# Three sets of seven-product column groups in each feed-forward unit of a one-core two-stack transformer

## The chip, the cores and the metric

One core of a Trainium2 chip runs one program. The metric is the device time of that program in microseconds; inputs lie in the chip's memory (HBM) and every weight is read once. TensorE multiplies, ScalarE and VectorE round, copy, gate and add, GpSimd does small work, SyncE's queue loads the weights.

## What is computed

The reference runs two small stacks one after the other over 256 rows of width 1024, in float32: mixers (attention, state-space scan, gated recurrence, MLA, GQA) and behind each of the four of them a feed-forward unit, the part that the change is about. The first stack's unit is, cut to its core:

```python
def swiglu(x, w_gate, w_up, w_down):
    return (jax.nn.silu(x @ w_gate) * (x @ w_up)) @ w_down
x = x + rms_norm(swiglu(rms_norm(x, norm_ffn_pre), w_gate, w_up, w_down), norm_ffn_post)
```

with a hidden width of 2816. The second stack's units have the same three products. All products are wanted to nearly float32.

## The kernel before, in words

**Products.** A float32 product is made of three in fp32r: each operand is rounded to a high part, and the rest is kept as a low part; `mm3` (L520) issues high x high, high x low and low x high (L521 to L523), each with 128 rows, 128 of the contraction and 512 columns. Below, "a product" is these three matmuls.

**Weights.** All weight matrices are packed into chunks of 128 x 2048 numbers in the order of use. SyncE loads chunk c into RAW[c % 3] (`weights`, L3072). ScalarE rounds it into WH[c % 3] (`split_hi`, L1364), VectorE subtracts to get the rest in WL[c % 3] (`split_lo`, L2050). On both engines `feed(c)` (L1366, L2052) makes all splits up to chunk c + 3 that aren't made yet, each as soon as TensorE has counted the chunk three before it as done (`S.used`). Where a `feed` stands among an engine's other work is written out by hand, and each engine works strictly in that order. TensorE waits for the rest of a chunk with `rests_ready` (L492).

**A feed-forward unit** (`ffn`, L832 on TensorE, L1467 on ScalarE, L2223 on VectorE) goes over 11 groups of 256 hidden columns, gate and up side by side, 512 columns of a PSUM bank for each half t of the rows. A plain group is two chunks of 8 products. ScalarE then applies Silu (`tanh`, L1471), VectorE multiplies (`gate`, L2227) into AN, and TensorE transposes AN in a `fold` (L836; four transposes) that ScalarE and VectorE copy out as high and low part (L1491, L2250). For g in FAST = (2, 4, 6, 8) a fold also makes sums of quarters: ScalarE keeps one quarter (`kept`, L1487), VectorE does five small operations (`form_sums`, L2236), ScalarE copies twice. Then the down projection (`wide_mm`) takes 11 chunks.

**Sets.** SETS = (2, 6): groups a and a + 1 are computed together from four chunks cs[2a] to cs[2a+3]. Each of two of these chunks ("fast" chunks, those in FASTS) is done with 7 products instead of 8, by sums of blocks of the activations (`forms`, L2264, once a unit) and of the weights (`sums`, L2117: four VectorE operations of 512 columns in YG; rounded by ScalarE in `sums_hi`, L1432; their rests in `sums_lo`, L2132). A fast chunk's split leaves out its first 512 columns. `set_mm` (L756) goes plain, fold, fast, plain, fast. The seven products go to separate banks, and VectorE puts them together with eight operations of 512 columns (`combine_first`, `combine_second`, L2156 and L2170).

**Order by hand.** On each engine `column_set(a)` (L1516, L2294) holds the set's work, and the end of `ffn` calls it between groups and folds. The fold ahead of the set stands at its head, in front of `feed(cs[2a])`:

```python
                def column_set(a):
                    fold(a - 1)
                    feed(cs[2 * a])
                    sums_hi(cs[2 * a + 3])
                    feed(cs[2 * a + 1])
```

`decay_rates` (L2614), 28 operations on 128 x 8 numbers, is put behind groups 8, 9 and 10 of ffn 0; ScalarE needs the result in the gated recurrence (L1854), some 100 us later.

Of the kernel before, what the change touches and what calls it, by code (L numbers as in the profile page):

```python
# [267 lines left out]
def program(nc, A, PLAN, NCH):  # L268
# [10 lines left out]
    with top:  # L279
# [239 lines left out]
        def pe(e):  # L519
# [188 lines left out]
            def early_chunk(f, a, first, c):  # L708

                m, i = FASTS[c], 0 if first else 1  # L710
                GSh, GSl = FB[f][8:10]
                k = 2 if first else 6
                W = lambda n: (WH[:, c % NW, 512 * n:512 * n + 512], WL[:, c % NW, 512 * n:512 * n + 512])
                T = lambda n: (TGh[:, n, :], TGl[:, n, :])
                Y = lambda j, t: (HTh[:, k + j, 128 * t:128 * t + 128], HTl[:, k + j, 128 * t:128 * t + 128])
                S_ = lambda n: (GSh[:, i, 128 * n:128 * n + 128], GSl[:, i, 128 * n:128 * n + 128])

                def mul(b, x, w, own):
                    return mm3(PS[:, b, :], *x, *w, own and first, not first)

                def side(b, x, w):
                    tk = mul(b, x, w, False)
                    if not first:
                        tk.then_inc(S.ms, 1)

                def top_left():
                    return mul(5, Y(0, 0), W(1), True)

                def with_sum(b, n):
                    e.wait_ge(S.tlo, 4 * m + T_ORDER.index(n) + 1)  # L730
                    return mul(b, *((S_(0), S_(1), S_(2), Y(1, 1))[n], T(n)), n < 3)

                rests_ready(e, c)
                e.wait_ge(S.gsl, 2 * f + i + 1)
                if first:
                    side(0, Y(1, 0), W(2))
                    side(1, S_(3), W(3))
                    e.wait_ge(S.an, gt_n(f, a - 1, 1))
                    with_sum(6, 1).then_inc(S.tu, 1)
                    with_sum(7, 2).then_inc(S.tu, 1)  # L740
                    with_sum(2, 3)
                    e.wait_ge(S.ylo, fold_n(f, a - 2))
                    with_sum(4, 0).then_inc(S.tu, 1)
                    e.wait_ge(S.ylo, fold_n(f, a - 1))
                    tk = top_left()
                else:
                    top_left().then_inc(S.ms, 1)
                    with_sum(6, 1).then_inc(S.tu, 1)
                    with_sum(4, 0).then_inc(S.tu, 1)
                    side(0, Y(1, 0), W(2))  # L750
# [2405 lines left out]
```

## Time and profile before

| | |
|---|---|
| median of 3 runs | 1228.4 us (1227.89 to 1228.4) |
| profiled execution, its own time | 1228.27 us |
| its span, first to last instruction | 1226.4 us |
| TensorE matmul busy | 1219.6 us, 99% |
| VectorE, ScalarE busy | 1013.4 us, 83%; 751.4 us, 61% |
| GpSimd busy | 97.9 us, 8% |
| granted TensorE clock, mean | 1.000 |
| read from HBM | 216.64 MB, 177 GB/s |

Busy time is the time in which an engine has an instruction under way; TensorE's matmuls overlap, so that 99% says that it never stood still, not that it was at its peak. Instructions on ScalarE and VectorE overlap by some 0.1 us at their ends; the step from start to start is shorter than the duration. L numbers are lines of the kernel before.

### The profile page before, as it was taken

What the parts mean: (1) busy time and instruction counts of PE and PEld (TensorE: products, weight loads), DVE (VectorE), ACT (ScalarE), POOL (GpSimd) and SP (SyncE); (2) the same over time, 40 slices, a digit from 0 to 9 for tenths busy, and PEclk for the clock granted to TensorE, in tenths of its full rate; (3) what the DMA queues carried; (4) which work ended last, traced back from release to release, by engine and by line L of the source; (5) the groups of instructions that cost most, each with busy time, mean ns of one, the idle gap of its engine ahead of it and who ended that gap; (6) DMA issues with size and microseconds to landing.
All of it is one profiled execution on the core that took longest, in us unless ns stands there. A gap on an engine that the chain in (4) does not pass through costs nothing.

```text
span 1226.4 us, 16404 instructions
## 1 busy us (share of the span) xinstructions
PE 1219.6 (99%) x6284; PEld 1013.5 (83%) x6284; DVE 1013.4 (83%) x1436; ACT 751.4 (61%) x1154; POOL 97.9 (8%) x123
## 2 busy tenths in 40 slices
PE   9999999999999999999999999999999999999998
PEld 7778888888888888888888888888888888888887
DVE  8986999889788798878887756988888785989787
ACT  8875756555998655555687536465556643745552
POOL 2520000000100100000232000000001300000000
PEclk9999999999999999999999999999999999999999
DMA  8544455546654564645555234556455315464552
GB/s 342 154 142 138 173 207 187 206 172 206 205 195 169 187 206 172 237 174 206 198 187 172 69 104 145 203 178 230 172 206 190 133 35 206 173 211 166 206 189 86
DMA packets 32830, 218.75 MB, mean 178 GB/s; under 512 B 3936, under 2 KB 4576, under 8 KB 7408
## 3 DMA queue, kind: packets, MB, share of 16 engines
q1 hardware_dynamic: 30384, 210.32, 48.8%
q0 software_dynamic: 1648, 6.88, 2.2%
q8 instruction: 50, 0.82, 0.3%
q10 hardware_dynamic: 720, 0.50, 0.1%
q14 instruction: 28, 0.23, 0.1%
HBM read 216.64 MB, written 1.05 MB: 177 GB/s over the span
## 4 chain that ended last, share of the span: by engine, by line
PE 94%; DVE 4%; issue 1%; ACT 1%; DMA 0%; SPq 0%; DVEq 0%; ACTq 0%
PE PS L521 26%; PE PS L523 26%; PE PS L522 26%; PE PS L527 6%; PE PS L1022 2%; PE PS L1046 1%; PE PS L558 1%; PE PS L630 1%; PE PS L624 1%; PE PS L625 1%; PE PS L556 1%; PE PS L555 1%; DVE WL L2050 1%; DMA RAW<-in_w 0%; PE PS L963 0%
## 5 line engine op out<-in xcount | busy, mean ns | idle before, releaser
L2050 DVE TENSOR_TENSOR WL<-RAW,WH 128x2048 fp32r<-128x2048 f32 (+3 forms) x198 | 420.8, 2131 | 97.8 <-ACT WH L1364 97.8
L1364 ACT ACTIVATE WH<-RAW 128x2048 fp32r<-128x2048 f32 (+3 forms) x200 | 356.6, 1789 | 119.2 <-PE PS L523 119.1
L521 PE MATMUL PS<-WH,HTh 128*128 128x512 f32 (+1 forms) x752 | 296.9, 395 | 0.1
L523 PE MATMUL PS<-WH,HTl 128*128 128x512 f32 (+1 forms) x752 | 291.6, 388 | 0.0
L522 PE MATMUL PS<-WL,HTh 128*128 128x512 f32 (+1 forms) x752 | 291.3, 387 | 0.0
L523 PEld LDWEIGHTS PS<-WH,HTl 128*128 128x128 f32 x752 | 141.2, 188 | 29.4
L521 PEld LDWEIGHTS PS<-WH,HTh 128*128 128x128 f32 x752 | 141.3, 188 | 29.3 <-DVE WL L2050 1.1
L522 PEld LDWEIGHTS PS<-WL,HTh 128*128 128x128 f32 x752 | 141.4, 188 | 26.9
L521 PE MATMUL PS<-WH,YAh 128*128 128x512 f32 x354 | 139.9, 395 | 0.1
L523 PE MATMUL PS<-WH,YAl 128*128 128x512 f32 x354 | 138.0, 390 | 0.0
L522 PE MATMUL PS<-WL,YAh 128*128 128x512 f32 x354 | 137.8, 389 | 0.0
L2930 POOL TENSOR_SCALAR st<-st 128x2 f32<-128x2 f32 (+4 forms) x33 | 23.1, 699 | 741.1 <-ACT JK L1404 668.3
L523 PEld LDWEIGHTS PS<-WH,YAl 128*128 128x128 f32 x354 | 66.5, 188 | 14.1
L521 PEld LDWEIGHTS PS<-WH,YAh 128*128 128x128 f32 x354 | 66.5, 188 | 13.7 <-issue 0.5
L522 PEld LDWEIGHTS PS<-WL,YAh 128*128 128x128 f32 x354 | 66.5, 188 | 13.0
L1383 ACT ACTIVATE YAh<-PS 128x512 fp32r<-128x512 f32 x38 | 22.0, 596 | 54.3 <-PE PS L527 39.1
L1383 ACT ACTIVATE YBh<-YG 128x512 fp32r<-128x512 f32 x64 | 35.4, 625 | 28.4 <-DVE YG L2127 16.8
L1383 ACT ACTIVATE HTh<-PS,cst 128x128 fp32r<-128x128 f32 (+1 forms) x136 | 38.8, 379 | 21.7 <-PE PS L527 21.7
L2069 DVE SCALAR_TENSOR_TENSOR HTl<-PS,cst,HTh 128x128 fp32r<-128x128 f32 (+1 forms) x136 | 38.7, 350 | 10.7 <-ACT HTh L1383 10.6
L521 PE MATMUL PS<-WH,YBh 128*128 128x512 f32 x112 | 43.9, 392 | 0.0
L523 PE MATMUL PS<-WH,YBl 128*128 128x512 f32 x112 | 43.6, 389 | 0.0
L522 PE MATMUL PS<-WL,YBh 128*128 128x512 f32 x112 | 43.6, 389 | 0.0
(546 smaller groups left out, 2051.0 us busy)
## 6 DMA issues: line engine op xcount, KB each, us to landing
RAW<-in_w SPq DMA_DIRECT2D x196, 1024.0 KB, 4.9
WL<-in_w POOLq DMA_DIRECT2D x2, 1024.0 KB, 9.0
BC<-in_rows POOLq DMA_DIRECT2D x4, 512.0 KB, 4.1
YG<-in_mem POOLq DMA_DIRECT2D x4, 512.0 KB, 4.9
X<-in_x SPq DMA_DIRECT2D x2, 512.0 KB, 5.4
RAW<-in_w SPq DMA_DIRECT2D x4, 256.0 KB, 5.7
BC<-in_s SPq DMA_DIRECT2D x1, 512.0 KB, 11.3
YG<-in_s SPq DMA_DIRECT2D x1, 512.0 KB, 9.2
```

What stands on the lines that cost most here:

```text
L521: e.matmul(out, ah, bh, start=start, stop=False, skip_group_check=joined)
L522: e.matmul(out, ah, bl, start=False, stop=False, skip_group_check=joined)
L523: return e.matmul(out, al, bh, start=False, stop=stop, skip_group_check=joined)
L527: return e.transpose(out, src, ident[0:p, 0:p])
L555: e.matmul(out, HTh[:, k, ts], WH[:, c % NW, w], start=k == 0, stop=False)
L556: e.matmul(out, HTh[:, k, ts], WL[:, c % NW, w], start=False, stop=False)
L1022: tk = e.matmul(PS[:, h % 2, 256 * t:256 * t + 256], q[:, 128 * t:128 * t + 128], k[:, 0:256], start=i == 0, stop=i == len(parts) - 1)
L1364: e.activation(WH[:, c % NW, w], RAW[:, c % NR, w], ACT.Copy).then_inc(S.hi, 1)
L1383: return e.activation(out, src, ACT.Copy, scale=scale)
L2050: e.tensor_tensor(WL[:, c % NW, w], RAW[:, c % NR, w], WH[:, c % NW, w].bitcast(f32), SUB).then_inc(S.lo, 1)
L2069: return e.scalar_tensor_tensor(out, src, gain, hi.bitcast(f32), MUL, SUB)
L2930: e.tensor_scalar(st[:, at:at + n], st[:, at:at + n], 1e-6, None, ADD).then_inc(S.var, 1)
```

## The change

There are three sets, at groups 2, 5 and 8, in place of two. In a set the first two chunks are the fast ones and the last two plain. The seven products of a fast chunk are no longer put together at the end: partial sums go on growing in four banks over all four chunks. ScalarE copies a bank to another (`cu`, `cv`) and one to SBUF (`c7`), VectorE adds twice (`j1`, `j2`), and TensorE adds its next products on top. The weights' sums are made in two steps: two for each fast chunk ahead of the set (`set_raw`), and two each, late, within it (`late_raw`); they are rounded by ScalarE into the free first 512 columns of WH and into YBh. The fold within a set moves from behind the first chunk to between the third and the fourth; folds of a group lie between its two chunks, and each fold has a bank of its own (FOLD_BANK). The load into RAW of chunk cs[2a+3] waits for the sixth operation on a set's weights, that of cs[2a+4] for the eighth. `decay_rates` moves out of ffn 0 to between the steps behind it. The diff, cut to its core:

```diff
 NF = len(FAST)
-SETS = (2, 6)
+SETS = (2, 5, 8)
 NS = 2 * len(SETS)
-BANKS = ((0, 1), (6, 7), (0, 2), (1, 3), (6, 7), (2, 3), (0, 2), (1, 3), (6, 7), (0, 1), (6, 7))
+BANKS = ((0, 1), (6, 7), (4, 2), (5, 3), (6, 7), (0, 2), (1, 3), (4, 5), (6, 2), (7, 3), (4, 5))
+FOLD_BANK = (0, 1, 4, 5, 6, 0, 1, 4, 6, 7, 4)
 EV_OUT = (0, 2, 4, 6)
 OUT0 = (0, 2, 8, 10, 4, 6)
...
     return 11 * f + g + 1
...
 TSh, TSl = (a[:, :, :].rearrange("p (n a) c -> p n (a c)", a=2) for a in (HTh, HTl))
-TGh, TGl = (a[:, 0:8, :].rearrange("p (n a) c -> p n (a c)", a=2) for a in (YBh, YBl))
+def set_t(f, a, i, j):
+    c, k = PLAN[FFNS[f]][2 * a + i], 6 + 2 * i
...
+def set_mm(f, a, cs, folds):
+    n, m0 = set_n(f, a), 4 * FASTS[cs[0]]
+    C11, C21 = BANKS[a]
+    C12, C22 = BANKS[a + 1]
     GSh, GSl = FB[f][8:10]
...
+    def W(i, w):
+        o, c = slice(512 * w, 512 * w + 512), cs[i]
+        return WH[:, c % NW, o], WL[:, c % NW, o]
+    def Y(i, j, t):
+        k, ts = 2 * i + j, slice(128 * t, 128 * t + 128)
+        return HTh[:, k, ts], HTl[:, k, ts]
+    def sum_of(i, q):
+        w = slice(128 * q, 128 * q + 128)
+        return GSh[:, i, w], GSl[:, i, w]
+    def add(b, x, w, start=False, stop=False):
+        return mm3(PS[:, b, :], *x, *w, start, stop, not (start or stop))
+    def T(i, j, ready):
+        e.wait_ge(S.tlo, m0 + ready)
+        return set_t(f, a, i, j)
+    def rows(c, k, t, half, b):
+        o = (k % 2) * 1024 + half * 512
+        return product(c, PS[:, b, :], (HTh, HTl), k, t, slice(o, o + 512), False, k == 7, True)
+    def bank_free(b):
+        for g in in_bank(a, b):
+            e.wait_ge(S.ylo, fold_n(f, g))
+    rests_ready(e, cs[0])
+    bank_free(C11)
+    add(C11, Y(0, 0, 0), W(0, 1), start=True)
+    rests_ready(e, cs[1])
+    add(C11, Y(1, 0, 0), W(1, 1), stop=True).then_inc(S.qa, 1)
+    e.wait_ge(S.gsl, 2 * f + 2)
+    bank_free(C12)
+    add(C12, sum_of(0, 2), T(0, 0, 1), start=True).then_inc(S.qt, 1)
+    add(C12, sum_of(1, 2), T(1, 0, 3), stop=True).then_inc(S.qt, 1)
+    e.wait_ge(S.cu, n + 1)
+    add(C22, sum_of(0, 1), T(0, 1, 2)).then_inc(S.qt, 1)
+    add(C22, sum_of(1, 1), T(1, 1, 4)).then_inc(S.qt, 1)
+    add(C11, Y(0, 1, 0), W(0, 2))
+    add(C11, Y(1, 1, 0), W(1, 2))
+    e.wait_ge(S.j1, n + 1)
+    add(C22, sum_of(0, 0), T(0, 0, 5))
+    add(C22, sum_of(1, 0), T(1, 0, 6)).then_inc(S.qc, 1)
+    rests_ready(e, cs[2])
+    for t, b in enumerate((C11, C21)):
+        for k in (4, 5):
+            rows(cs[2], k, t, 0, b)
+    e.wait_ge(S.cv, n + 1)
+    add(C12, sum_of(0, 3), W(0, 3)).then_inc(S.used, 1)
+    add(C12, sum_of(1, 3), W(1, 3)).then_inc(S.used, 1)
+    add(C21, Y(0, 1, 1), T(0, 1, 7))
+    add(C21, Y(1, 1, 1), T(1, 1, 8))
+    e.wait_ge(S.j2, n + 1)
+    for t, b in enumerate((C12, C22)):
+        for k in (4, 5):
+            tk = rows(cs[2], k, t, 1, b)
     tk.then_inc(S.used, 1)
...
     folds()
...
+    rests_ready(e, cs[3])
+    for t in range(2):
+        for k in (6, 7):
+            for half in range(2):
+                tk = rows(cs[3], k, t, half, BANKS[a + half][t])
+    tk.then_inc(S.used, 1)
...
+def group(g, folds=None):
     for n, c in enumerate(cs[2 * g:2 * g + 2]):
+        if n and folds:
+            folds()
         rests_ready(e, c)
...
+        for t, b in enumerate(BANKS[g]):
             if n == 0:
...
+                free(g, b)
             for k in range(4 * n, 4 * n + 4):
                 w = slice(512 * (k % 4), 512 * (k % 4) + 512)
...
+                tk = product(c, PS[:, b, :], (HTh, HTl), k, t, w, k == 0, k == 7)
         tk.then_inc(S.used, 1)
+def two_folds(g):
+    fold(g)
...
 edge_mm(cs[0:2], 4, 512, BANKS[0], ed)
 group(1)
 fold(0)
 set_mm(f, 2, cs[4:8], lambda: fold(1))
-group(4)
-fold(2)
-fold(3)
-group(5)
-fold(4)
-set_mm(f, 6, cs[12:16], lambda: fold(5))
-group(8)
-fold(6)
-fold(7)
-group(9)
-fold(8)
-group(10)
-fold(9)
+group(4, lambda: two_folds(2))
+set_mm(f, 5, cs[10:14], lambda: fold(4))
+group(7, lambda: two_folds(5))
+set_mm(f, 8, cs[16:20], lambda: fold(7))
+group(10, lambda: two_folds(8))
...
+def column_set(a, *folds):
+    n = set_n(f, a)
+    C11, C12, C22 = BANKS[a][0], *BANKS[a + 1]
+    feed(cs[2 * a - 1])
+    e.wait_ge(S.qa, n + 1)
+    if a > SETS[0]:
+        e.wait_ge(S.an, gt_n(f, [g for g in range(a) if C22 in BANKS[g]][-1], 1))
+    copy(PS[:, C22, :], PS[:, C11, :]).then_inc(S.cu, 1)
+    e.wait_ge(S.qt, 4 * n + 2)
+    copy(FB[f][5][:, 3, :], PS[:, C12, :]).then_inc(S.c7, 1)
+    late_hi(a, 0, 0)
+    late_hi(a, 1, 0)
+    tanh(a - 1)
+    e.wait_ge(S.qc, n + 1)
+    copy(PS[:, C12, :], PS[:, C22, :]).then_inc(S.cv, 1)
+    late_hi(a, 0, 1)
+    late_hi(a, 1, 1)
+    for g in folds:
+        fold(g)
     feed(cs[2 * a])
-    sums_hi(cs[2 * a + 3])
     feed(cs[2 * a + 1])
-    n = SETS.index(a)
-    e.wait_ge(S.ms, 9 * f + 3 * n + 1)
-    copy(FB[f][5][:, 2, :], PS[:, 5, :]).then_inc(S.eo, 1)
     feed(cs[2 * a + 2])
     tanh(a)
     tanh(a + 1)
...
 feed(cs[2])
-tanh(1)
-fold(0)
-sums_hi(cs[5])
-feed(cs[3])
-column_set(2)
-group(4, 2, 3)
-feed(cs[10])
-sums_hi(cs[13])
-tanh(5)
-kept(4)
-feed(cs[11])
-fold(4, True)
-column_set(6)
-group(8, 6, 7)
-group(9, 8)
-group(10, 9)
+set_hi(2, 1)
+column_set(2, 0, 1)
+set_hi(5, 0)
+fold(2)
+fold(3)
+feed(cs[8])
+set_hi(5, 1)
+column_set(5, 4)
+set_hi(8, 0)
+fold(5)
+fold(6)
+feed(cs[14])
+set_hi(8, 1)
+column_set(8, 7)
+fold(8)
+fold(9)
+feed(cs[20])
+feed(cs[21])
+tanh(10)
 if f < 3:
...
+def set_raw(a, i):
+    c, m0 = cs[2 * a + i], 4 * FASTS[cs[2 * a]]
+    B12, B11, B21, B22 = (RAW[:, c % NR, 512 * n:512 * n + 512] for n in range(4))
+    if m0 and i == 0:
+        e.wait_ge(S.tlo, m0)
+    e.tensor_tensor(TR_[:, 2 * i, :], B22, B12, SUB).then_inc(S.tr, 1)
+    e.wait_ge(S.tr, m0 + 2 * i + 1)
+    e.tensor_tensor(TR_[:, 2 * i + 1, :], TR_[:, 2 * i, :], B11, ADD).then_inc(S.tr, 1)
...
+def late_raw(a, i, j):
+    c, m0 = cs[2 * a + i], 4 * FASTS[cs[2 * a]]
+    B12, B11, B21, B22 = (RAW[:, c % NR, 512 * n:512 * n + 512] for n in range(4))
+    e.wait_ge(S.tlo, m0 + 2 * i + j + 1)
+    if j == 0:
+        e.tensor_tensor(TR_[:, 2 * i, :], B12, B11, SUB).then_inc(S.tr, 1)
+    else:
+        e.tensor_tensor(TR_[:, 2 * i + 1, :], B21, TR_[:, 2 * i + 1, :], SUB).then_inc(S.tr, 1)
...
+def column_set(a, *folds):
+    n = set_n(f, a)
+    C21, C22, M7 = BANKS[a][1], BANKS[a + 1][1], FB[f][5][:, 3, :]
+    late_raw(a, 0, 0)
+    late_raw(a, 0, 1)
+    late_raw(a, 1, 0)
+    feed(cs[2 * a - 1])
+    set_rest(a, 5, 0, 0)
+    e.wait_ge(S.c7, n + 1)
+    e.wait_ge(S.qt, 4 * n + 4)
+    e.tensor_tensor(PS[:, C21, :], PS[:, C22, :], M7, ADD).then_inc(S.j1, 1)
+    set_rest(a, 6, 1, 0)
+    late_raw(a, 1, 1)
+    gate(a - 1)
+    e.wait_ge(S.cv, n + 1)
+    e.tensor_tensor(PS[:, C22, :], PS[:, C22, :], M7, ADD).then_inc(S.j2, 1)
+    set_rest(a, 7, 0, 1)
+    set_rest(a, 8, 1, 1)
+    for g in folds:
+        fold(g)
     feed(cs[2 * a])
-    sums_lo(c)
     feed(cs[2 * a + 1])
-    combine_first(f, n, c)
-    combine_second(f, n, c, lambda: feed(cs[2 * a + 2]))
+    feed(cs[2 * a + 2])
     gate(a)
     gate(a + 1)
-    feed(c)
+    feed(cs[2 * a + 3])
...
 gate(0)
 feed(cs[1])
+set_raw(2, 0)
 forms_lo()
+set_rest(2, 1, 0, 0)
+set_rest(2, 2, 0, 1)
 feed(cs[2])
-sums(cs[5])
-fold(0)
-gate(1)
-sums_lo(cs[5])
-feed(cs[3])
-fold(1)
-column_set(2)
-group(4, 2, 3)
-sums(cs[13])
-feed(cs[10])
-gate(5)
-form_sums(4)
-sums_lo(cs[13])
-fold(4, True)
+set_ahead(2, 1)
+column_set(2, 0, 1)
+set_ahead(5, 0)
+fold(2)
+fold(3)
+feed(cs[8])
+set_ahead(5, 1)
+column_set(5, 4)
+set_ahead(8, 0)
 fold(5)
-feed(cs[11])
-column_set(6)
-group(8, 6, 7)
-if beside:
-    for g in (2, 3, 4):
-        beside(g)
-group(9, 8)
-if beside:
-    beside(5)
-    beside(6)
-group(10, 9)
-if beside:
-    beside(7)
-    beside(8)
+fold(6)
+feed(cs[14])
+set_ahead(8, 1)
+column_set(8, 7)
+fold(8)
+fold(9)
+feed(cs[20])
+feed(cs[21])
+gate(10)
...
-ffn(0, 1, decay_rates)
...
 edge_mm(PLAN["od0"], 2)
+decay_rates(2)
+decay_rates(3)
 feed(PLAN["od0"][1])
 conv(0)
 mem_lo(0)
+decay_rates(4)
 feed(PLAN["od1"][0])
 conv(1)
+decay_rates(5)
 feed(PLAN["od1"][1])
 conv_lo(0)
 conv(2)
 conv(3)
+decay_rates(6)
+decay_rates(7)
 feed(PLAN["mem00"][0])
 conv_lo(1)
+decay_rates(8)
 feed(PLAN["mem00"][1])
 head_sum("memk0", JK2, 128)
 feed(PLAN["rg0"][0])
...
     if c - NR in FASTS:
-        e.wait_ge(S.tr, 4 * FASTS[c - NR] + 4)
+        m = FASTS[c - NR]
+        e.wait_ge(S.tr, 4 * m + (4 if m % len(FAST_AT) >= NS or m % 2 else 6))
     e.dma_start(RAW[:, c % NR, :], A["w"][c]).then_inc((S.w0, S.w1, S.w2)[c % NR], 16)
...
```

## Rows read from the trace of the kernel before

**Rows 1.** The page, busy time, share of the span and instructions of each engine.
```profile
PE 1219.6 (99%) x6284; PEld 1013.5 (83%) x6284; DVE 1013.4 (83%) x1436; ACT 751.4 (61%) x1154; POOL 97.9 (8%) x123
```

**Rows 2.** The page, the chain that ended last, shares of the span by engine.
```profile
PE 94%; DVE 4%; issue 1%; ACT 1%; DMA 0%; SPq 0%; DVEq 0%; ACTq 0%
```

**Rows 3.** Who waited for whom: total us, times, longest us; all engines, then PEld.
```profile
ACT WH L1364 <- PE PS L523: 119.1, 53, 3.5
DVE WL L2050 <- ACT WH L1364: 97.8, 94, 3.1
...
PEld PS L527 <- issue: 2.3, 7, 0.3
PEld PS L570 <- ACT WH L1364: 1.6, 4, 0.6
```

**Rows 4.** Timeline of PE in ffn 1: start us, us, instruction, xcount.
```profile
431.65 0.39 PE L521 MATMUL PS<-WH,HTh 128*128 128x512 f32 x1
...
435.73 0.60 PE L527 MATMUL PS<-ident,ffn1AN 128*128 128x128 f32 x4
436.09 0.47 PE L521 MATMUL PS<-WH,HTh 128*128 128x512 f32 x1
```

**Rows 5.** Groups by form, ScalarE: xcount, busy us, mean ns, idle before.
```profile
L1364 ACT ACTIVATE WH<-RAW 128x1536 fp32r<-128x1536 f32 x32 | 47.6, 1489 | 21.0 <-PE PS L523 21.0
```

**Rows 6.** Groups by form, VectorE.
```profile
L2050 DVE TENSOR_TENSOR WL<-RAW,WH 128x1536 fp32r<-128x1536 f32 x32 | 56.1, 1755 | 9.1 <-ACT WH L1364 9.1
...
L2068 DVE TENSOR_TENSOR YBl<-YG,YBh 128x512 fp32r<-128x512 f32 x64 | 39.8, 683 | 0.0
...
L2152 DVE TENSOR_TENSOR PS<-PS,ffn1TS 128x512 f32<-128x512 f32 x10 | 6.6, 692 | 0.0
```

**Rows 7.** Timeline of ScalarE, then of VectorE, round fold 2 of ffn 1.
```profile
468.41 1.92 ACT L1364 ACTIVATE WH<-RAW 128x2048 fp32r<-128x2048 f32 x1 [2.01 <-PE PS L523]
470.23 0.26 ACT L1383 ACTIVATE JK<-PS 128x128 f32<-128x128 f32 x1
474.13 0.60 ACT L1383 ACTIVATE YAh<-PS 128x512 fp32r<-128x512 f32 x1 [3.65 <-DVE JK L2248]
474.63 0.52 ACT L1383 ACTIVATE ffn1SFh<-JK 128x384 fp32r<-128x384 f32 x1
475.04 0.59 ACT L1383 ACTIVATE YAh<-PS 128x512 fp32r<-128x512 f32 x1
475.52 0.84 ACT L1485 ACTIVATE ffn1TS<-PS,st 128x256 f32<-128x256 f32 x2
...
470.36 2.29 DVE L2050 TENSOR_TENSOR WL<-RAW,WH 128x2048 fp32r<-128x2048 f32 x1 [1.23 <-ACT WH L1364]
472.57 0.28 DVE L2240 TENSOR_TENSOR JK<-PS,JK 128x128 f32<-128x128 f32 x1
...
473.81 0.29 DVE L2248 TENSOR_TENSOR JK<-PS,JK 128x128 f32<-128x128 f32 x1
```

**Rows 8.** Timeline of ScalarE, then of VectorE, ahead of the set at 2.
```profile
429.25 3.29 ACT L1364 ACTIVATE WH<-RAW 128x2048 fp32r<-128x2048 f32 x2
...
430.04 0.87 DVE L2233 SCALAR_TENSOR_TENSOR ffn1AN<-PS,st,ffn1TS 128x256 f32<-128x256 f32 x2
```

**Rows 9.** PE at the program's start; a window: busy of PE to POOL, clock.
```profile
1.44 4.11 PE L563 MATMUL PS<-YBh 128*128 128x512 f32 x9 [1.44 <-DVE YBh L2385]
...
6.18 1.39 PE L563 MATMUL PS<-YBh 128*128 128x512 f32 x5
...
0.00:5.00 5.00, 3.56 (x8) 2.81 (x9) 0.48 (x1) 1.59 (x3) 0.50 (x8) 1.00 0.64 180
```

**Rows 10.** A `series` line: ns min/median/max; then a window behind ffn 0, as above.
```profile
L2610 DVE TENSOR_TENSOR lm<-lm x8: 156/167/168, 233.9 to 251.7; 128x8 f32<-128x8 f32 x8
...
312.00:340.00 28.00, 28.00 (x143) 23.47 (x142) 22.61 (x34) 27.94 (x45) 2.99 (x7) 1.00 0.61 207
```

**Rows 11.** The page, DMA issues: xcount, KB each, us to landing.
```profile
RAW<-in_w SPq DMA_DIRECT2D x196, 1024.0 KB, 4.9
```

More of the change, by code:

```diff
@@ L706, in fast_chunk @@
                 mul(2, Y(1, 1), T(3), False).then_inc(S.used, 1)
-            def early_chunk(f, a, first, c):
-                m, i = FASTS[c], 0 if first else 1
+            def set_mm(f, a, cs, folds):
+                n, m0 = set_n(f, a), 4 * FASTS[cs[0]]
+                C11, C21 = BANKS[a]
+                C12, C22 = BANKS[a + 1]
                 GSh, GSl = FB[f][8:10]
[L712 to L750, printed above, removed]
-                    side(1, S_(3), W(3))
-                    with_sum(7, 2).then_inc(S.tu, 1)
-                    tk = with_sum(2, 3)
-                tk.then_inc(S.used, 1)
@@ L756, in set_mm @@
-            def set_mm(f, a, cs, folds):
-                def plain(c, k0):
-                    rests_ready(e, c)
-                    for t in range(2):
-                        if k0 == 0:
-                            e.wait_ge(S.an, gt_n(f, a - 1 if a > 2 and t else a - 2, 1))
-                        for k in (k0, k0 + 1):
-                            for half in range(2):
-                                o = (k % 2) * 1024 + half * 512
-                                tk = product(c, PS[:, 2 * t + half, :], (HTh, HTl), k, t, slice(o, o + 512), k == 0,
-                                             k == 5 and t == 1 and half == 1)
-                    tk.then_inc(S.used, 1)
-                plain(cs[0], 0)
-                folds()
-                early_chunk(f, a, True, cs[1])
-                plain(cs[2], 4)
-                early_chunk(f, a, False, cs[3])
+                def W(i, w):
+                    o, c = slice(512 * w, 512 * w + 512), cs[i]
+                    return WH[:, c % NW, o], WL[:, c % NW, o]
@@ L1488, in kept, with fold @@
                     e.wait_ge(S.fold, fold_n(f, g))
-                    copy(SR[:, g % 2, 384:512], PS[:, 4 + g % 2, 128:256]).then_inc(S.sa, 1)
-                def fold(g, ahead=False):
+                    copy(SR[:, g % 2, 384:512], PS[:, FOLD_BANK[g], 128:256]).then_inc(S.sa, 1)
+                def fold(g):
                     hi, lo, j = ydst(f, 2 * g)
@@ L1494, in fold @@
                         n = FAST.index(g)
-                        if not ahead:
-                            kept(g)
+                        kept(g)
                         e.wait_ge(S.sr, 3 * (NF * f + n) + 3)
-                        copy(hi[:, j:j + 2, :], pair(4 + g % 2)).then_inc(S.yhi, 1)
+                        copy(hi[:, j:j + 2, :], pair(FOLD_BANK[g])).then_inc(S.yhi, 1)
                         copy(FB[f][6][:, n, :], SR[:, g % 2, 0:384]).then_inc(S.sfh, 1)
@@ L2134, in sums_lo, with joins @@
                 m = FASTS[c]
-                hi, lo = (TGh, TGl) if early(c) else (TSh, TSl)
                 for q, n in enumerate(T_ORDER):
                     e.wait_ge(S.thi, 4 * m + q + 1)
-                    rest(lo[:, n, :], TR_[:, n, :], hi[:, n, :]).then_inc(S.tlo, 1)
-            def joins(f, n):
-                cb, TS = joined(f, n), FB[f][5]
-                if n == 2:
-                    E1, U, V, Q = (TS[:, i, :] for i in range(4))
-                else:
-                    E1, U, V = TS[:, 2, :], TS[:, 3, :], JK[:, 512:1024]
-                    Q = U
+                    rest(TSl[:, n, :], TR_[:, n, :], TSh[:, n, :]).then_inc(S.tlo, 1)
+            def joins(f):
+                cb, TS = 8 * f, FB[f][5]
+                E1, U, V, Q = (TS[:, i, :] for i in range(4))
                 def join(out, b, a, after=0):
@@ L2154, in joins, with combine_first @@
                 return join, E1, U, V, Q
[L2156 to L2160 removed]
+            def combine_first(f):
+                m = NF * f + NF - 1
+                join, E1, U, V, Q = joins(f)
+                e.wait_ge(S.eo, f + 1)
                 e.wait_ge(S.tu, 3 * m + 1)
```

131 lines of the change are left out of this document (62 added, 69 removed).

## Prediction

> **What bounds the kernel now.** I read the page's busy shares first: TensorE's matmuls fill 1219.6 of the 1226.4 us [rows 1]. The chain that ended last is 94% TensorE [rows 2], and the waits of its two rows (matmul and weight load) are all under 2.5 us in total [rows 3]. So TensorE never waits for more than 0.6 us but for its start, and the time is its number of products. VectorE (1013 us busy) and ScalarE (751 us) do wait, 97.8 us for L1364 and 119.1 us for TensorE [rows 1, 3]; they stand close behind it, and every step that they make one after another while TensorE has nothing to do is time lost. The order of the change is therefore the thing to read.
>
> The sum is made against the profiled execution, 1228.27 us with its ends, 0.1 us below the median of the three runs, 1228.4. A measurement of this kernel can tell some 0.2%, 2.5 us, from no change.
>
> **What it removes.** From 431.65 to 435.73 TensorE starts 18 matmuls [rows 4], 0.227 us each; one product is three of them, 0.68 us. A set takes 14 + 8 + 8 = 30 products in both kernels in place of 32. Three sets instead of two in each of four ffn calls save 4 x 2 x 3 = 24 matmuls: **-5.4 us**. The six joins per set that go (0.69 us each [rows 6]) and the two joins that come lie on VectorE and count only in the chains below.
>
> **Cost one: the last chunk of a set.** TensorE does the set's third chunk, then the fold (`folds()`), then waits for the weights of the fourth, cs[2a+3]. On ScalarE and VectorE the split of that chunk is `feed(cs[2a])`, and it now stands behind that same fold; the feed before it reaches only cs[2a+2]. So nothing can hide it: fold, copy, split, rest are one chain with TensorE at its head. Before, the fold stood behind the first chunk, with two chunks to cover it. With steps from the start of one to the start of the next where the engine goes on by itself: the four transposes take 0.60, of which 0.36 pass before TensorE could go on [rows 4], so 0.24; ScalarE's copy of 512 columns 0.50; its split 1.91; VectorE's rest of 2048 columns 2.29; four handoffs of 0.03 (the split ends at 470.33, the rest starts at 470.36) [rows 4, 7]. 0.24 + 0.50 + 1.91 + 2.29 + 0.12 = **5.0 us** for the sets at 2 (fold 1) and 8 (fold 7). At 5 it is fold 4, one of FAST: in between come the kept copy 0.26, VectorE's five small operations, 472.57 to 474.10, 1.53, the second copy 0.41 and two more handoffs [rows 7]: **7.3 us**. Together 17.3 per ffn, **+69.2 us**. Bounds: without any handoff 0.15 less a wait, with full durations in place of steps 0.2 more; no gain is possible in a chain that starts at TensorE's own fold.
>
> **Cost two: the first two chunks of a set.** Both are now fast chunks and stand at its head, so all sums and their roundings are wanted at once. I call L the time at which the rest of the second fast chunk is there. VectorE starts an instruction 0.08 us before the end of the one ahead (2.21 after a 2.29) [rows 7], so a step of 512 columns is 0.60 [rows 6]. From L it does in order: two sums and two rests, 2.7 us with the waits for ScalarE's roundings between them; three late sums 3 x 0.60; the rest of cs[2a+2] 2.21; one rest 0.60; the join for `j1` 0.69 [rows 6]. That is L + 8.0. TensorE wants `j1` after eight products, 5.5 us from the start of the set. (ScalarE's chain, split of cs[2a+2] and the copy `cu`, ends at L + 4.4 and makes TensorE wait on the way; `j1` comes later and decides.) So a set loses (L - start) + 2.5.
>
> L for the set at 2, in the times of ffn 1 [rows 8]: the gates end at 430.8 and ScalarE has split cs[4] by then (1.49 from 429.25); its rest, 1536 columns, 1.67 -> 432.5 [rows 5, 6]; two sums 1.3; the two rests of `forms` 1.2; two rests 1.2; the rest of cs[5] 1.75 -> 437.9. TensorE would start at 436.09 [rows 4]. It loses 1.8 + 2.5 = 4.3.
> L for the set at 5, from the start of the last chunk of the set at 2: that chunk ends at 5.4; ScalarE's four Silu (0.4 a step) start at 5.6 and end at 7.2, its 1536-column split at 8.7; VectorE's rest at 10.5; two sums and two rests, 13.0; the five small operations of fold 2, 14.5; three copies 0.50 + 0.41 + 0.50, 16.0; split 1.49, 17.5; rest 1.75, L = 19.2 [rows 5 to 7]. TensorE does two more chunks (10.9) and two folds (0.36 each) [rows 4] and would start at 17.1. It loses 2.1 + 2.5 = 4.6. For the set at 8 folds 5 and 6 come the other way round: 0.1 more, 4.7. Together 13.6 per ffn, **+54.4 us**. Bounds: if L were early, one chain is left from the start of the set, split 1.91, rest 2.29, rest 0.60 and join 0.69, 5.65 with its handoffs against 5.5, so not under 0.15 a set, 2 us in all; above, a handoff of 0.1 more at ten steps a set makes 12 us more. I take the worked-out value, as every step has a row of the same form.
>
> **Cost three: TensorE's clock.** TensorE never rests for long in this trace, so what 5 to 7 us do to it isn't shown. The nearest row is the start of the program: nine matmuls of 512 columns from 1.44 on take 4.11 us, one every 0.46 us, which is the pace of 1.2 GHz, though the granted clock is recorded as 1.00; the five from 6.18 start every 0.25, the pace of 2.4 GHz [rows 9]. One such restart costs 9 x (0.46 - 0.23) = 2.1 us. Twelve long waits: between nothing and 12 x 2.1 = 25 us. I take it for the four waits of 7.3 us and half of the eight of 5.0, 8 x 2.1 = **+17 us**, since the one rest that the trace shows ended slow. The Trainium skill ("TensorE: Matmul & The Clock Gate", Part 1) says that the chip halves the array's clock after idling and gives it back only after sustained work; it speaks against this change, and by it all long waits could be charged, 25 us in place of 17, the trace agreeing in its one case.
>
> **What costs nothing.** The 28 small operations of `decay_rates` (0.17 us each [rows 10], 4.8 us) leave idle time of ffn 0 and go in behind it, between 313 and 345 us; from 312 to 340 VectorE is busy 22.6 of 28 us and TensorE all of it [rows 10]; what hides them is that a chunk lasts TensorE 5.4 us and a rest 2.3. Without that cover, 5 us. On SP's queue the load of cs[2a+3] now waits for the sixth sum and that of cs[2a+4] for the eighth; a load lands in 4.9 us [rows 11], and both are wanted over 8 us after their sums. The down projection starts with two plain chunks (10.9 us), which cover the two folds moved ahead of its first splits: nothing, up to 2 us. POOL is not touched.
>
> **Sum.** 1228.3 - 5.4 + 69.2 + 54.4 + 17 = 1363.5; I say **1363 us**.
>
> **Rivals.**
> - *The clock stays up.* The long waits don't slow the restart: 1363 - 17 = **1346 us**. For it: the granted clock is 1.00 all along. Against: rows 9. Chance 0.20.
> - *The head of a set is covered.* If the sums come early enough for all but 0.2 us a set, only cost one is left: 1228.3 - 5.4 + 69.2 + 2 = 1294, with the clock's part up to **1311 us**. Against: the chain of 19.2 us above, which has no slack. Chance 0.12.
> - *Waits and clock feed each other.* The clock falls at all twelve waits, each slow stretch lasts twice as long (4.2 us of loss), and handoffs add 12: 1346 + 50 + 12 = 1408 at the far end, **1385 us** in its middle. For: a slow chunk moves the Silu and the next fold back by its whole loss. Chance 0.15.
> - *The other side.* If `feed` for cs[2a+3] were done by the time TensorE leaves the fold, only the saved products would be left: 1228.3 - 5.4 = **1222.9 us**. Its place is that one split; it decides as soon as a set loses less than 5.4 / 12 = 0.45 us in all. Against it stands the program order itself: 4.2 us of ScalarE and VectorE follow the fold. Chance 0.03.
>
> **How the numbers follow.** The forecast as worked out has 0.50. The range takes in the forecast, the case without the clock and most of the case above: 1318 to 1396 us. It leaves out the other side, the covered head but for its upper edge, and the far end. Slower by over 0.2%: 0.96; faster: 0.03; within: 0.01.
>
> **What would show it.** TensorE's busy share falls to about 90%, and VectorE -> TensorE waits appear that weren't there: four of about 7 us and eight of about 5 us of a weight load for the rest of a 2048-column chunk (what L2050 does now), each right behind a fold; and per set some four shorter ones, 0.5 to 2 us, for the rest of the second fast chunk, a T's rest, ScalarE's bank copy and the join. The matmul count falls by 24. After the long waits a few matmuls start 0.43 to 0.47 us apart if the clock falls. No new wait at 313 to 345 us. The prediction is wrong in cost one if TensorE goes from the fold to the fourth chunk in under 4 us, in cost two if a set's first eight products take under 8 us.

## The result and the profile after

The changed kernel takes **1374.47 us** (median of 4 runs, 1373.04 to 1377.77) against 1228.29 us: 1.1195 times the time before, interval 1.1173 to 1.1216. Forecast were 1363 us, in a range of 1318 to 1396. The profiled execution took 1373.56 us, 145.3 more than that of before. Three executions, of two of the experiments, ran at a mean granted clock of 0.74 to 0.85 and took 6 to 17% longer; they are left out of every time and trace below.

The page of the changed kernel, busy time and chain, the lines that answer to [rows 1] and [rows 2]:

```profile
PE 1257.7 (92%) x6260; PEld 1025.5 (75%) x6260; DVE 1029.4 (75%) x1460; ACT 780.8 (57%) x1214; POOL 98.1 (7%) x123
...
PEclk9999999999999998999999999989999999999999
...
PE 67%; DVE 19%; ACT 9%; issue 4%; DMA 0%; SPq 0%; DVEq 0%; ACTq 0%
```

TensorE has 24 matmuls fewer and is busy for 92% of the span instead of 99%. VectorE's share fell too, from 83% to 75%, with 16 us more of work: it isn't the bound by its load. The chain that ended last is TensorE for 67% only; in the rest it runs over VectorE and ScalarE, engines that TensorE waited for. PEclk shows 8 in two slices.

Lines have moved: L521 to L523 are now L525 to L527, the fold's transposes L531, ScalarE's split L1367, VectorE's rest of a chunk L2077, the other rests L2095, the join `j1` L2351. What the weight loads waited for (engine, line, releaser: total us, times, longest):

```profile
PEld PS L525 <- DVE WL L2077: 87.8, 28, 7.3
PEld PS L525 <- ACT PS L1386: 20.4, 12, 1.7
PEld PS L525 <- DVE PS L2351: 11.4, 11, 1.0
PEld PS L525 <- DVE WL L2095: 9.9, 12, 0.8
```

In [rows 3] the largest total of a weight load's waits was 2.3 us. Now there are four larger ones: the rest of a chunk (28 times: twelve long ones, the last chunks of the sets, and sixteen short ones), the bank copy `cu`, the join `j1` and the rests of the weights' sums.

**The wait behind a fold.** The set at 2 in ffn 1. Timelines of TensorE, of ScalarE and of VectorE (start us, us, instruction, count, idle before it and its releaser):

```profile
493.27 0.60 PE L531 MATMUL PS<-ident,ffn1AN 128*128 128x128 f32 x4
498.67 0.79 PE L525 MATMUL PS<-WH,HTh 128*128 128x512 f32 x1 [4.81 <-DVE WL L2077]
...
500.12 0.63 PE L525 MATMUL PS<-WH,HTh 128*128 128x512 f32 x1
500.54 0.63 PE L526 MATMUL PS<-WL,HTh 128*128 128x512 f32 x1
...
503.10 0.52 PE L526 MATMUL PS<-WL,HTh 128*128 128x512 f32 x1
503.46 0.39 PE L527 MATMUL PS<-WH,HTl 128*128 128x512 f32 x1
503.69 0.39 PE L525 MATMUL PS<-WH,HTh 128*128 128x512 f32 x1
...
493.90 0.60 ACT L1386 ACTIVATE YAh<-PS 128x512 fp32r<-128x512 f32 x1 [6.56 <-PE PS L531]
494.39 5.50 ACT L1367 ACTIVATE WH<-RAW 128x2048 fp32r<-128x2048 f32 x3
...
494.53 0.69 DVE L2095 TENSOR_TENSOR YAl<-PS,YAh 128x512 fp32r<-128x512 f32 x1 [6.21 <-ACT YAh L1386]
496.33 4.49 DVE L2077 TENSOR_TENSOR WL<-RAW,WH 128x2048 fp32r<-128x2048 f32 x2 [1.11 <-ACT WH L1367]
```

The four transposes start at 493.27; the next product, on the fourth chunk, at 498.67. Between stand just the steps of the forecast: ScalarE idles until the transposes end and copies (493.90), splits (from 494.39, three chunks in one go, of which the first is the one wanted), and VectorE, which has made the fold's low part by 495.22 and then idles until 496.33, makes the rest. TensorE loses 498.67 - 493.27 - 0.36 = 5.04 us. The set at 5, with fold 4, the same views:

```profile
537.97 0.60 PE L531 MATMUL PS<-ident,ffn1AN 128*128 128x128 f32 x4
...
545.67 0.79 PE L525 MATMUL PS<-WH,HTh 128*128 128x512 f32 x1 [7.10 <-DVE WL L2077]
...
538.61 0.28 ACT L1386 ACTIVATE JK<-PS 128x128 f32<-128x128 f32 x1 [7.05 <-PE PS L531]
540.49 0.60 ACT L1386 ACTIVATE YAh<-PS 128x512 fp32r<-128x512 f32 x1 [1.61 <-DVE JK L2265]
...
543.33 6.69 DVE L2077 TENSOR_TENSOR WL<-RAW,WH 128x2048 fp32r<-128x2048 f32 x3 [1.05 <-ACT WH L1367]
```

Here the kept copy and the five small operations come first: 545.67 - 537.97 - 0.36 = 7.34 us.

**The restart.** The matmuls behind the 5 us wait start 0.43 us apart (500.12 to 500.54 above) until 503.10 and 0.23 from 503.46 on: the pace of 1.2 GHz, then of 2.4. The granted clock agrees (windows of the changed kernel; the column behind POOL's is PEclk, a mean over the window; from 498.50 to 503.30 alone it is 0.50):

```profile
495.00:500.00 5.00, 1.33 (x3) 1.14 (x4) 3.89 (x3) 4.89 (x3) 0.00 (x0) 0.65 0.17 23
500.00:505.00 5.00, 5.00 (x16) 3.93 (x16) 3.02 (x2) 0.00 (x0) 0.00 (x0) 0.66 0.92 367
505.00:510.00 5.00, 5.00 (x24) 4.14 (x23) 2.05 (x5) 2.94 (x5) 0.00 (x0) 1.00 0.68 243
```

All twelve long waits are followed by such a slow stretch, of 6 to 13 matmuls. Against 0.23 us a matmul, and the 0.1 us that any resumption costs, they lose 1.3 to 2.6 us, 24.5 in all. A thirteenth stretch, 1.6 us, stands behind a wait of only 1.27 us for the copy, at 850.96. Together 26.1 us.

**The head of a set.** VectorE in the set at 2 of ffn 1, from the second chunk's rest (L = 475.52) to the join; then TensorE's first product of the set and the one that waited for the join:

```profile
473.77 1.75 DVE L2077 TENSOR_TENSOR WL<-RAW,WH 128x1536 fp32r<-128x1536 f32 x1
475.44 0.68 DVE L2316 TENSOR_TENSOR YG<-RAW 128x512 f32<-128x512 f32 x1
...
482.17 0.68 DVE L2095 TENSOR_TENSOR WL<-YG,WH 128x512 fp32r<-128x512 f32 x1
482.77 0.69 DVE L2351 TENSOR_TENSOR PS<-PS,ffn1TS 128x512 f32<-128x512 f32 x1
...
473.65 0.47 PE L525 MATMUL PS<-WH,HTh 128*128 128x512 f32 x1
...
475.58 0.51 PE L525 MATMUL PS<-WH,HTh 128*128 128x512 f32 x1 [0.99 <-DVE WL L2077]
475.92 0.40 PE L526 MATMUL PS<-WL,HTh 128*128 128x512 f32 x1
...
483.52 0.51 PE L525 MATMUL PS<-WH,ffn1GSh 128*128 128x512 f32 x1 [0.61 <-DVE PS L2351]
```

L is 475.5, `j1` ends at 483.46, L + 7.9. The product that needs it starts 9.87 us after the set's first (473.65), where the eight products take 5.5: 4.35 us lost. In the same way the set at 5 lost 4.5 and that at 8 lost 4.6 us. (The weight load of that product waited longer than the matmul, as it is issued ahead of it: both views occur below.)

### The profile page after: what moved, and what is told of

It is laid out like the page before. It is cut to its first block, busy times and chain, and to the rows that moved or that the text cites. A ratio compares the mean times of both kernels' runs of the same rounds, so it can differ in the third digit from the quotient of the medians.

```text
span 1371.7 us, 16449 instructions
## 1 busy us (share of the span) xinstructions
PE 1257.7 (92%) x6260; PEld 1025.5 (75%) x6260; DVE 1029.4 (75%) x1460; ACT 780.8 (57%) x1214; POOL 98.1 (7%) x123
## 4 chain that ended last, share of the span: by engine, by line
PE 67%; DVE 19%; ACT 9%; issue 4%; DMA 0%; SPq 0%; DVEq 0%; ACTq 0%
PE PS L525 19%; PE PS L527 19%; PE PS L526 19%; DVE WL L2077 6%; ACT WH L1367 4%; PE PS L531 4%; DVE WL L2095 2%; PE PS L1025 2%; PE PS L1049 1%; DVE YBl L2095 1%; DVE YG L2332 1%; ACT WH L1386 1%; ACT HTh L1386 1%; DVE YG L2316 1%; ACT JK L1407 1%
## 5 line engine op out<-in xcount | busy, mean ns | idle before, releaser
L2077 DVE TENSOR_TENSOR WL<-RAW,WH 128x2048 fp32r<-128x2048 f32 (+3 forms) x198 | 415.1, 2110 | 94.1 <-ACT WH L1367 94.0
L1367 ACT ACTIVATE WH<-RAW 128x2048 fp32r<-128x2048 f32 (+3 forms) x200 | 351.1, 1768 | 89.7 <-PE PS L527 89.6
L525 PE MATMUL PS<-WH,HTh 128*128 128x512 f32 (+1 forms) x704 | 291.9, 415 | 79.2 <-DVE WL L2077 79.2
L526 PE MATMUL PS<-WL,HTh 128*128 128x512 f32 (+1 forms) x704 | 282.8, 402 | 0.0
L527 PE MATMUL PS<-WH,HTl 128*128 128x512 f32 (+1 forms) x704 | 281.9, 400 | 0.0
L525 PEld LDWEIGHTS PS<-WH,HTh 128*128 128x128 f32 x704 | 138.9, 197 | 116.1 <-DVE WL L2077 87.8
L527 PEld LDWEIGHTS PS<-WH,HTl 128*128 128x128 f32 x704 | 138.3, 196 | 30.3
L525 PE MATMUL PS<-WH,YAh 128*128 128x512 f32 x354 | 139.5, 394 | 0.1
L527 PE MATMUL PS<-WH,YAl 128*128 128x512 f32 x354 | 138.0, 390 | 0.0
L527 PEld LDWEIGHTS PS<-WH,YAl 128*128 128x128 f32 x354 | 66.5, 188 | 14.0
L525 PEld LDWEIGHTS PS<-WH,YAh 128*128 128x128 f32 x354 | 66.5, 188 | 13.8 <-issue 0.5
L1386 ACT ACTIVATE WH<-YG 128x512 fp32r<-128x512 f32 x48 | 28.8, 626 | 60.8 <-DVE YG L2316 40.9
L2095 DVE TENSOR_TENSOR YAl<-PS,YAh 128x512 fp32r<-128x512 f32 x38 | 25.6, 686 | 42.7 <-ACT YAh L1386 42.7
L525 PE MATMUL PS<-WH,YBh 128*128 128x512 f32 x112 | 43.9, 392 | 0.0
L527 PE MATMUL PS<-WH,YBl 128*128 128x512 f32 x112 | 43.6, 389 | 0.0
```

The costliest lines, as they stand in the source:

```text
L525: e.matmul(out, ah, bh, start=start, stop=False, skip_group_check=joined)
L526: e.matmul(out, ah, bl, start=False, stop=False, skip_group_check=joined)
L527: return e.matmul(out, al, bh, start=False, stop=stop, skip_group_check=joined)
L1367: e.activation(WH[:, c % NW, w], RAW[:, c % NR, w], ACT.Copy).then_inc(S.hi, 1)
L1386: return e.activation(out, src, ACT.Copy, scale=scale)
L2077: e.tensor_tensor(WL[:, c % NW, w], RAW[:, c % NR, w], WH[:, c % NW, w].bitcast(f32), SUB).then_inc(S.lo, 1)
```

## The experiments

All are edits of the changed kernel, in the order in which they teach, not in which they ran. None leaves out work; the busy wait (e2) adds some. The names are those of the expectations' labels (e1 to e10); e6 and e9 are the kernels of e1 and e5 run a second time, to have a trace of them.

**The fourth chunk is split ahead of the fold** (on ScalarE and on VectorE):

```diff
                     late_hi(a, 1, 1)
-                    for g in folds:
-                        fold(g)
                     feed(cs[2 * a])
+                    for g in folds:
+                        fold(g)
```

> Edit: in a set, ScalarE and VectorE split the fourth chunk, cs[2a+3], before they copy the fold out; TensorE's order stays. Theory (the three costs add up): the twelve waits behind the folds, 69 us, go to under 0.5 us each, and the slow restarts behind them, 2.0 to 2.7 us each and 26 us in all, go with them; 1374 - 69 - 26 = 1279 us, up to 1285. The waits at the heads of the sets stay at 4.3 to 4.7 us a set. Rival (the wait only moves): the fold copied later holds back the next chunks' splits and the next set's sums, so the heads of the sets wait longer and more than 20 us of the 95 come back: above 1300 us.

Measured: 1288.44 us (three executions, 1287.7 to 1292.94), ratio to the kernel before 1.0499 (1.0478 to 1.052). Some 86 us of the 146 are gone. That is 9 us above the theory's 1279 and above its upper end, 1285, but well below the rival's 1300, which is thereby out. The trace of the second run was to show what the 9 us are. (Its expectation puts e1 at 1290.7 us, the median of all its four executions.)

> Edit: the same as e1_feed_first, for a profile that is not disturbed. Theory: of the 1290.7 us some 8 are waits that e1's expectation left out: with the split of the fourth chunk ahead of the fold, the split of the chunk after it is still behind it, and at 5, where the fold is long, TensorE waits some 1.1 us for it (4 times, 5 us); heads as in the changed kernel, no slow restart, 1288 us. Rival: there are slow restarts behind waits of 1 to 2 us, 2 us each, at several places.

Measured: 1288.89 us. TensorE's waits for the rest of a chunk, of this kernel:

```profile
PEld PS L525 <- DVE WL L2077: 27.4, 19, 2.1
```

They came down from 87.8 to 27.4 us. Each ffn has a wait of 1.65 us behind the set at 5 (the expectation said 1.1), as the following chunk's split still stands behind the long fold 4: 6.6 us. Four slow stretches are left, 6.3 us, none of them behind the rest of a chunk: each follows one of the twelve waits of 1.26 us for the copy. These two things, 12.9 us, are what lies above the theory's sum (12 us in the profiled execution). So this expectation's rival, slow stretches behind short waits, came true beside its theory. The twelve long waits are gone with their slow stretches: moving one line takes back 86 us, in e1 and in e6.

**Busy while waiting.** TensorE multiplies into an unused bank behind the fold:

```diff
                 folds()
+                for _ in range(27 if a == 5 else 17):
+                    e.matmul(PS[:, BANKS[a - 1][1], :], HTh[:, 0, 0:128],
+                             HTh[:, 0:2, :].rearrange("p a b -> p (a b)"), start=True, stop=True)
                 rests_ready(e, cs[3])
```

> Edit: behind the fold within a set TensorE makes products into a bank that nobody reads until it is started anew, 17 matmuls of 512 columns (3.9 us) in the sets at 2 and 8 and 27 (6.1 us) at 5, and then waits for the fourth chunk as before. Theory (idle time alone lowers the clock): the split of the fourth chunk lands at the same time as before, TensorE's remaining wait is 1.2 us or less, its matmuls start 0.227 us apart right behind it, and the mean granted clock goes from 0.969 to 1.000; the time falls by the slow restarts, 12 x 2.2 = 26 us, to 1348 us (1345 to 1352). Rival (the slow matmuls come from taking up work after a semaphore or from a fresh chunk, not from idleness): the time stays at 1374 us or rises.

Measured: 1351.51 us (1349.34 to 1352.79), ratio 1.1 (1.0984 to 1.1017); mean granted clock 0.994. The same place in ffn 1, TensorE's timeline:

```profile
488.80 0.60 PE L531 MATMUL PS<-ident,ffn1AN 128*128 128x128 f32 x4
489.15 4.12 PE L779 MATMUL PS<-HTh 128*128 128x512 f32 x17
494.22 0.50 PE L525 MATMUL PS<-WH,HTh 128*128 128x512 f32 x1 [0.94 <-DVE WL L2079]
494.55 0.39 PE L526 MATMUL PS<-WL,HTh 128*128 128x512 f32 x1
494.78 0.40 PE L527 MATMUL PS<-WH,HTl 128*128 128x512 f32 x1
495.02 0.39 PE L525 MATMUL PS<-WH,HTh 128*128 128x512 f32 x1
```

From the fold (488.80) to the fourth chunk (494.22) pass 5.42 us; in the changed kernel it was 5.40. The weights come no sooner, the wait that is left is 0.94 us, and the matmuls behind it start 0.23 us apart. The slow stretches fell from thirteen to five (each behind a copy's wait of 1.27 us) and from 26.1 to 7.9 us, and the joins' waits by 2.4 us, as a slow stretch no longer moves the next head's chain back: 20.6 of the 21.8 us between the profiled executions. So TensorE paid for having been idle, and not for the semaphore or the fresh chunk: with useless work it was faster than without.

**A shorter idle time.** The fold within a set goes four products earlier, in front of the last half of the third chunk (on TensorE alone):

```diff
                 e.wait_ge(S.j2, n + 1)
+                folds()
                 for t, b in enumerate((C12, C22)):
...
-                folds()
                 rests_ready(e, cs[3])
```

> Edit: TensorE does the fold within a set four products (12 matmuls, 2.7 us) earlier, before the second half of the third chunk; nothing else moves. Theory: each of the twelve waits shrinks by 2.7 us, from 5.0 to 2.3 and from 7.3 to 4.6 us: 12 x 2.7 = 33 us less. Of the slow restarts those behind the eight waits of 2.3 us may go, 8 x 2.2 = 17 us more: 1324 us if they go, 1341 us if they stay. Rival (the wait is not the chain that starts at the fold but the load or the free buffer of the fourth chunk): the waits keep their length and the time stays at 1374 us.

Measured: 1337.28 us, ratio 1.0885 (1.0869 to 1.0901). The wait in the set at 2 of ffn 1:

```profile
482.79 0.60 PE L531 MATMUL PS<-ident,ffn1AN 128*128 128x128 f32 x4
...
488.20 0.66 PE L525 MATMUL PS<-WH,HTh 128*128 128x512 f32 x1 [2.07 <-DVE WL L2077]
```

It is 2.07 us where it was 4.81 (these idle times count from the modelled end of the last matmul), 2.74 less, so the wait is the chain that starts at the fold, and the rival is out. The first matmul behind it is 0.66 us long, already slow. All eight waits of 2.07 us and all four that are left of the long ones (4.36 us, at 5) were still followed by a slow stretch, and so were three of the copy's: fifteen, 24.9 us. The slow stretch thus stayed with the shorter idle time of 2.07 us; in front of the fourth chunk it is gone where 0.94 us of idling are left (e2) and where none are (e6). The profiled execution is 35.4 us shorter, of which 12 x 2.74 = 32.9 are the waits' part, 1.2 the stretches' and 1.2 the joins'.

**Which wait of the head decides.** ScalarE makes the bank copy before the third chunk's split:

```diff
-                    feed(cs[2 * a - 1])
                     e.wait_ge(S.qa, n + 1)
...
                     copy(PS[:, C22, :], PS[:, C11, :]).then_inc(S.cu, 1)
+                    feed(cs[2 * a - 1])
```

> Edit: at the head of a set ScalarE makes the bank copy (cu) before it splits the third chunk, in place of after it. Theory (the join j1 decides, at the end of VectorE's chain): TensorE's twelve waits of 1.7 us for the copy, 20 us in the trace, fall to some 0.2 us each, and the waits for the join grow by as much; the time stays at 1374 us (1371 to 1377). Rival (the waits of the head add up, each is a cost of its own): the time falls by 12 x 1.5 = 18 us to 1356 us.

Measured: 1378.89 us (1377.47 to 1380.57), ratio 1.1228. TensorE's waits in this kernel:

```profile
PEld PS L525 <- DVE WL L2077: 87.8, 28, 7.3
PEld PS L525 <- DVE PS L2351: 30.8, 12, 2.6
```

The copy's 20.4 us are off the list, and the join has 30.8 instead of 11.4. A wait that isn't the last of its head gives nothing when it goes; the rival's 18 us didn't come. The kernel is even 4 us slower than the changed one, a little outside the forecast 1377. The matmul that needs the join now idles 2.14 us where before it and the copy's idled 1.27 and 0.61, 3 us more in twelve heads, though with one resumption less in each (1.2 us); and there are fourteen slow stretches, 29.5 us, 3.4 more: two of the twelve idle times of 2.14 us were followed by one (at 856.01 and 1186.58).

**The folds behind the heads.** As the first edit, and

```diff
                 set_ahead(5, 0)
-                fold(2)
-                fold(3)
                 feed(cs[8])
                 set_ahead(5, 1)
-                column_set(5, 4)
+                column_set(5, 2, 3, 4)
```

with the same for folds 5 and 6 at the set at 8, on ScalarE too, and `feed(cs[2 * a + 1])` ahead of the folds. Besides, the kept copy and the small operations of folds 4, 6 and 8 now wait for the fold two groups before.

> Edit: as e1_feed_first, and the next chunk's split too goes ahead of the fold; the copies of folds 2, 3 and 5, 6 on ScalarE and VectorE move from ahead of the sets at 5 and 8 to behind their heads, beside folds 4 and 7. Theory (the rest of the second fast chunk comes late because of these folds): the heads at 5 and 8 lose 1.0 us each in place of 4.5 and 4.6, 8 x 3.5 = 28 us, and the wait of 1.1 us at 5 goes, 5 us; the head at 2 stays at 4.3: 1289 - 33 = 1256 us. Rival (VectorE has no room: folds put off hold back the splits behind the set): waits appear behind the sets and the time stays above 1270 us.

Measured: 1270.1 us, ratio 1.0341 (1.0324 to 1.0359), at the edge of the rival's "above 1270". 19 of the 33 us came, against e6, and 6.3 of those of the profiled execution (20.3) because it has no slow stretch left. TensorE's waits by its matmuls, of this kernel:

```profile
PE PS L525 <- ACT PS L1386: 10.1, 8, 1.3
PE PS L525 <- DVE PS L2351: 7.1, 12, 0.6
...
PE PS L525 <- DVE WL L2075: 2.9, 6, 1.0
...
PE PS L531 <- DVE ffn1AN L2248: 1.4, 1, 1.4
```

The heads at 5 did shrink as forecast, from a loss of 4.55 us to 0.85: in ffn 1 it has a wait of 0.55 us for `j1` and no other. The head at 8 shrank by 1.1 us only, from 4.65 us in the changed kernel to 3.56, where 1.0 was forecast. Its wait for the rest of the second fast chunk fell from 1.34 us to 0.25, but those of 0.40 (a rest), 1.26 (the copy) and 0.61 us (`j1`) are as before (TensorE in the set at 8 of ffn 1, first of the changed kernel, then of this one):

```profile
567.75 0.50 PE L525 MATMUL PS<-WH,HTh 128*128 128x512 f32 x1 [1.34 <-DVE WL L2077]
...
522.74 0.50 PE L525 MATMUL PS<-WH,HTh 128*128 128x512 f32 x1 [0.25 <-DVE WL L2075]
```

The set's first product starts at 565.57 and at 521.65, so L comes 2.2 us behind the start in the one kernel and 1.1 in the other. With 2.5 us for the rest of the chain, as the prediction has it, that makes losses of 4.7 and 3.6 us. The formula held where L moved. And each ffn has a new wait of 1.4 us: the transposes in the group behind the set at 5 wait for VectorE's gate (L2248). Why L is still late at 8, and not at 5, wasn't tried.

**Products ahead of the join.** As the last one, and

```diff
+                rests_ready(e, cs[2])
+                for k in (4, 5):
+                    rows(cs[2], k, 0, 0, C11)
                 e.wait_ge(S.j1, n + 1)
...
-                for t, b in enumerate((C11, C21)):
-                    for k in (4, 5):
-                        rows(cs[2], k, t, 0, b)
+                for k in (4, 5):
+                    rows(cs[2], k, 1, 0, C21)
```

> Edit: as e7_head_first, and TensorE makes two of the third chunk's products, those into C11, before it waits for the join j1, in place of after it. Theory (j1 decides the head, products between cover it): each head loses up to 1.36 us less: at 2 from 4.3 to 2.9, at 5 and 8 from 1.0 to 0.1: 4 x (1.4 + 2 x 0.9) = 13 us less than e7, 1243 us. Rival (the rest of the third chunk, which these products need, lands no earlier than the join): the time stays that of e7.

Measured: 1265.35 us (1262.54 to 1266.95), ratio 1.0299. The waits for `j1`, 7.1 us in the view above, are gone from the list, but only 5 of the forecast 13 us came. Where no slow stretch falls into a head, it lost 0.74 to 0.84 us less than in e7: the wait for `j1` and the resumption behind it, which was all that there was to cover, and not the 1.4 us forecast for the head at 2. That is 9 us in twelve heads. The copy's waits stand at 9.7 us after 10.1: they come before these products, which can't cover them. And three slow stretches are back, 4 to 5 us, two behind the copy's 1.26 us and one behind the gate's 1.44. It is the best version found, and 3% above the kernel before.

**The decay rates back in ffn 0**, behind the set at 8:

```diff
-            ffn(0, 1)
+            ffn(0, 1, decay_rates)
```

> Edit: the small operations of the decay rates go back into ffn 0, behind the set at 8; the rest is the changed kernel. Theory (moving them wasn't free): in the changed kernel ScalarE waits 1.41 us for the last of them at 386 us and TensorE 1.30 us at once; both waits go, and the stretch from the last L527 product with ffn0SFl to the first fold of ffn 1 shrinks from 144.3 to the 142.2 us that it had before; the total falls by 2 us to 1372.4 us, which is inside the spread of the changed kernel's own runs (1373.0 to 1377.8), so the stretch decides. Rival (as predicted: they cost nothing there, the 2 us come from elsewhere): the stretch stays at 144.3 us.

Measured: 1375.3 us (two executions).

> Edit: the same as e5_decay_back, for an undisturbed profile. The stretch from the last L527 product with ffn0SFl to the first fold of ffn 1 is 144.3 us in the changed kernel, in e6, e7 and e8, and 142.2 us in the kernel before. Theory: 142.2 us, and no wait of ScalarE for the small operations. Rival: 144.3 us.

Measured again: 1374.03 us (1372.9 to 1375.15). In the changed kernel ScalarE waits for the last of the small operations (waits from 380 to 392 us):

```profile
ACT TR L1827 <- DVE lm L2690: 1.4, 1, 1.4
PE PS L525 <- issue: 1.3, 1, 1.3
```

The last four of them stand in VectorE's order behind the convolutions (4.8 us from 376.29), the rest of a chunk and a low part (382.62 to 385.95). With the operations back this is gone, and the stretch from the last product with ffn0SFl to the first fold of ffn 1 is 142.4 us in place of 144.3. But the total stays. The waits of TensorE from 250 to 330 us of that kernel say why:

```profile
PE PS L525 <- DVE WL L2077: 4.8, 1, 4.8
PE PS L525 <- DVE HTl L2095: 1.7, 1, 1.7
```

The operations now delay the rest of an activation (HTl) by 1.7 us at the start of the down projection. The same in the best version:

> Edit: e8_rows_early with the decay rates back in ffn 0. Theory: the stretch falls from 144.3 to 142.2 us and nothing else moves: 1265.4 - 2 = 1263 us. Rival: in ffn 0 the small operations (4.8 us) now stand in VectorE's way, as it was freed of folds there only to be late for them: the time stays at 1265 us or rises.

Measured: 1266.52 us (1264.78 to 1268.32): no gain, with a wait of 2.6 us for HTl in ffn 0, followed by a slow stretch. The stretch behind ffn 0 did fall, to 142.5 us. So the rival was right about the total; how much of it is the operations' isn't shown, as this trace has seven slow stretches and that of e8 three.

## Why the prediction was right, point by point

- *What bounds it*: as read. TensorE had no slack, and VectorE and ScalarE are bounds by the length of their chains, not by their load.
- *What it removes*: 6284 - 6260 = 24 matmuls, as counted.
- *Cost one*, forecast 5.0 (its terms add up to 5.06) and 7.3 us, 69.2 in all: measured 5.04 and 7.34, 8 x 5.04 + 4 x 7.34 = 69.7 us. Shown by the feed moved ahead of the fold and by the fold moved ahead of four products.
- *Cost two*, forecast 4.3, 4.6 and 4.7 us per ffn: measured 4.35, 4.5 and 4.6 in ffn 1, so about 4 x 13.4 = 54 us. In ffn 2 and 3 the first wait of the head at 2 is missing, 2 us less. That the join decides is shown by the copy made first, and that a loss goes with L by the head at 8 in e7.
- *What costs nothing*: wrong for the decay rates. The step was the cover, "a chunk lasts TensorE 5.4 us and a rest 2.3": it looked at the weights' rests, but not at VectorE's convolutions behind them. They and the gates of the recurrence that ScalarE makes of them are one chain with the small operations, and it reaches TensorE: 2 us, at 386 us (350 in the kernel before's times, 5 us behind the place that the prediction named). Left in ffn 0 they would have cost the changed kernel as much (e9). The rest held: no wait for the queue of the loads, none of two or more us at the down projection.
- *Sum*: -5.4 + 69.7 + 54 - 2 + 26.1 + 2 = 144.4, measured 145.3. Of the 10 us between the forecast and the profiled execution, the clock's part is 9 and the decay rates' 2, less the 2 us of the heads in ffn 2 and 3.
- *Rivals*: a clock that stays up and covered heads would have given 1346 and 1311 us and are both excluded, as is the other side, 1222.9 us. (The range was said to take in the upper edge of the covered heads; 1311 lies below its 1318.) Of the case with waits and clock feeding each other the clock's half came true, without stretches twice as long.
